# Two transformer blocks on one core: the FFN gate copied ahead of up, the sum of squares split, two weight splits swapped

## What is computed

```
def swiglu(h, w_gate, w_up, w_down):
    return (jax.nn.silu(h @ w_gate) * (h @ w_up)) @ w_down

def rms_norm(x, g):
    xf = x.astype(jnp.float32)
    y = xf * lax.rsqrt(jnp.mean(xf * xf, axis=-1, keepdims=True) + NORM_EPS)
    return (y * g.astype(jnp.float32)).astype(x.dtype)
...
        x = x + 0.5 * rms_norm(swiglu_2(rms_norm(x, g[0]), ffn_w_in[i, 0], ffn_w_out[i, 0]), g[1])
        ...
        x = x + rms_norm(m, g[3])
        x = x + 0.5 * rms_norm(swiglu_2(rms_norm(x, g[4]), ffn_w_in[i, 1], ffn_w_out[i, 1]), g[5])
```

## Time and profile before

| | |
|---|---|
| median of 3 runs | 2837.49 us (2835.84 to 2841.38) |
| the profiled execution | 2834.45 us, its span 2832.7 us |
| mean granted TensorE clock | 0.981 |
| busy: PE, DVE, ACT, POOL | 94%, 65%, 52%, 6% of the span |
| L671, L675 (in), L684 and L714 (out) | the FFN's matmuls |
| DVE L433 (`lo_a`) and L444 (`lo_b`) | 711.2 and 268.0 us busy |
| ACT L421 (`hi_a`) and L440 (`hi_b`) | 590.7 and 229.1 us busy |

### The profile page before, as it was taken

The page is one execution under the profiler, slowest core; times in us unless marked ns, Lnnn a source line. Parts: engine busy times, 40 slices in busy tenths (PEclk is TensorE's granted clock), DMA queues, the critical chain, the costliest instruction groups (busy, mean ns, idle before and its releaser), DMA issues.

```text
span 2832.7 us, 43885 instructions
## 1 busy us (share of the span) xinstructions
PE 2675.4 (94%) x15554; PEld 2305.1 (81%) x15554; DVE 1844.0 (65%) x2617; ACT 1459.1 (52%) x2295; POOL 160.5 (6%) x231
## 2 busy tenths in 40 slices
PE   6899998999899989999998899999999999999998
PEld 6888888888788868888887578888887888887787
DVE  4766667666666676666664566676656666666665
ACT  3545445454454465555543554555555545455644
POOL 0000000000000030000000300000011000003000
PEclk9999998999999999999998999999999999999999
DMA  4346642466666536656654056756535665653664
GB/s 128 104 149 195 183 129 90 148 186 183 188 178 182 153 128 178 188 167 198 188 167 152 1 161 187 204 160 195 158 126 175 196 191 173 184 169 114 178 186 134
DMA packets 575822, 457.02 MB, mean 161 GB/s; under 512 B 19276, under 2 KB 537956, under 8 KB 575716
## 3 DMA queue, kind: packets, MB, share of 16 engines
q1 hardware_dynamic: 573124, 453.47, 54.0%
q10 hardware_dynamic: 2560, 2.10, 0.3%
q0 software_dynamic: 32, 0.02, 0.0%
HBM read 452.37 MB, written 1.07 MB: 160 GB/s over the span
## 4 chain that ended last, share of the span: by engine, by line
issue 79%; PE 8%; DVE 5%; ACT 2%; POOL 2%; DVEq 1%; POOLq 1%; DMA 1%; SPq 0%; ACTq 0%
DVE lo_a L433 2%; POOL arena L1138 1%; POOL small L2091 1%; ACT hi_a L421 1%; POOLq L2090 1%; PE gu L872 1%; DVE small L1105 1%; PE gu L874 1%; PE gu L873 1%; PE gu L1330 0%; DVEq L1467 0%; PE gu L880 0%; PE gu L879 0%; PE gu L878 0%; PE gu L1332 0%
## 5 line engine op out<-in xcount | busy, mean ns | idle before, releaser
L433 DVE TENSOR_TENSOR lo_a<-raw_a,hi_a 128x2048 fp32r<-128x2048 f32 (+1 forms) x313 | 711.2, 2272 | 387.2 <-ACT hi_a L421 385.8
L421 ACT ACTIVATE hi_a<-raw_a 128x2048 fp32r<-128x2048 f32 (+1 forms) x313 | 590.7, 1888 | 140.5 <-PE acc L1360 28.2
L671 PE MATMUL tp<-xT,hi_a 128*128 128x512 f32 x1760 | 441.3, 393 | 0.0
L671 PE MATMUL gu<-xT,hi_a 128*128 128x512 f32 x1600 | 397.9, 391 | 0.0
L671 PEld LDWEIGHTS tp<-xT,hi_a 128*128 128x128 f32 x1760 | 324.5, 189 | 62.5
L671 PEld LDWEIGHTS gu<-xT,hi_a 128*128 128x128 f32 x1600 | 294.0, 188 | 56.9
L684 PE MATMUL acc<-hi_b,h_hi 128*128 128x512 f32 x800 | 313.8, 392 | 0.0
L684 PE MATMUL acc<-lo_b,h_hi 128*128 128x512 f32 x800 | 313.7, 392 | 0.0
L684 PE MATMUL acc<-hi_b,h_lo 128*128 128x512 f32 x800 | 311.2, 389 | 0.0
L444 DVE TENSOR_TENSOR lo_b<-raw_b,hi_b 128x1024 fp32r<-128x1024 f32 x220 | 268.0, 1218 | 6.7 <-ACT hi_b L440 6.7
L675 PEld LDWEIGHTS tp<-xT,lo_a 128*128 128x128 f32 x1760 | 240.1, 191 | 30.1 <-DVE lo_a L433 13.6
(11 more groups left out here) (316 smaller groups left out, 4168.1 us busy)
## 6 DMA issues: line engine op xcount, KB each, us to landing
raw_a<-in_ffn_w_in SPq DMA_DIRECT2D x352, 512.0 KB, 5.6
raw_b<-in_ffn_w_out SPq DMA_DIRECT2D x176, 512.0 KB, 3.6
raw_a<-in_w_in SPq DMA_DIRECT2D x52, 512.0 KB, 4.8
raw_a<-in_w_gate SPq DMA_DIRECT2D x44, 512.0 KB, 4.8
raw_a<-in_w_up SPq DMA_DIRECT2D x44, 512.0 KB, 6.1
raw_b<-in_w_down SPq DMA_DIRECT2D x44, 512.0 KB, 3.6
raw_a<-in_w_out SPq DMA_DIRECT2D x24, 512.0 KB, 4.2
raw_a<-in_c_w_in SPq DMA_DIRECT2D x24, 512.0 KB, 4.6
```

The source lines that it names most:

```text
L421: nc.scalar.activation(a_view(hi_a, par)[:, :, 0:width], a_view(raw_a, par)[:, :, 0:width], ACT.Copy).then_inc(a_hi, 1)
L433: nc.vector.tensor_tensor(a_view(lo_a, par)[:, :, 0:width], a_view(raw_a, par)[:, :, 0:width], a_view(hi_a, par)[:, :, 0:width].bitcast(F3 ...
L671: nc.tensor.matmul(banks[:, e, :], w_hi[:, kt, e * P:(e + 1) * P], xT[:, :, kt, :], start=(kt == 0), stop=False)
```

## The change

Three edits.

1. In an FFN tile, the copy of both halves (L736) becomes two copies of 256 columns. ACT now waits for `gate_done`, which PE raises after the last gate matmul, copies the gate half, waits for the scaled gate, takes Silu, then waits for `a_used`, copies the up half and goes on as before. DVE waits for `gate_part` ahead of the gate add and for `up_part` ahead of the up add.
2. In `post_pool` and `post_act`, POOL adds eps to the first half's sum as soon as that half is squared; ACT, after its second square and the drain that was already there, adds the second half with a one-column Identity activation (bias as the other addend); POOL then only raises to -0.5.
3. In `pre_dve`, `lo_slot_a` of the second slot stands ahead of `lo_slot_b` of the first down slot.

```
@@ pre_dve @@
             ins.then_inc(diag_ready, 1)
+            ahead_a(lo_slot_a, dve, s.a0 + 1)
             if s.kind == "ffn":
                 lo_slot_b(dve, s.b0, 0)
-            ahead_a(lo_slot_a, dve, s.a0 + 1)
@@ post_act @@
                 act.drain()
+                act.wait_ge(post_part, 2 * s.post + t + 1)
+                nc.scalar.activation(msy[:, t:t + 1], ssy[:, 2 * t + 1:2 * t + 2], ACT.Identity, bias=ssy0[:, t:t + 1]).then_inc(post_sum, 1)
@@ first_products, and the same in ffn_in_pe @@
+                            if s.kind == "ffn" and part == 2 and kt == KT - 1 and e == 0:
+                                mm.then_inc(gate_done, 1)
@@ ffn_tile_act @@
-            act.wait_ge(a_used, n + 1)
+            act.wait_ge(gate_done, m + 1)
             if not isinstance(m, int) or m >= 2:
                 act.wait_ge(hid_ready, m - 1)
-            nc.scalar.activation(parts[:, pm, :, :], (gu, tp)[pm][:, :, 256:512], ACT.Copy).then_inc(hid_part, 1)
+            nc.scalar.activation(parts[:, pm, 0, :], (gu, tp)[pm][:, 0, 256:512], ACT.Copy).then_inc(gate_part, 1)
             act.wait_ge(hid_scaled, m + 1)
             nc.scalar.activation(sg[:, pm, :], gs[:, pm, :], ACT.Silu).then_inc(hid_gate, 1)
+            act.wait_ge(a_used, n + 1)
+            nc.scalar.activation(parts[:, pm, 1, :], (gu, tp)[pm][:, 1, 256:512], ACT.Copy).then_inc(up_part, 1)
             act.wait_ge(hid_ready, m + 1)
@@ ffn_tile_dve @@
-            dve.wait_ge(hid_part, m + 1)
+            dve.wait_ge(gate_part, m + 1)
             nc.vector.tensor_tensor(gs[:, pm, :], banks[:, 0, 0:256], parts[:, pm, 0, :], ALU.add)
             dve.drain()
             nc.vector.tensor_tensor(gs[:, pm, :], gs[:, pm, :], rb, ALU.mult).then_inc(hid_scaled, 1)
+            dve.wait_ge(up_part, m + 1)
             nc.vector.tensor_tensor(parts[:, pm, 1, :], banks[:, 1, 0:256], parts[:, pm, 1, :], ALU.add)
@@ post_pool @@
             for t in range(NT):
-                pool.wait_ge(post_sq, 4 * s.post + 2 * t + 2)
-                rsqrt_pool(pool, rstdy[:, t:t + 1], 2 + t, ssy[:, 2 * t:2 * t + 1], eps_y[:, t:t + 1] if s.kind == "ffn" else EPS2,
-                           ssy[:, 2 * t + 1:2 * t + 2]).then_inc(rstdy_ready, 1)
+                pool.wait_ge(post_sq, 4 * s.post + 2 * t + 1)
+                nc.gpsimd.tensor_scalar(ssy0[:, t:t + 1], ssy[:, 2 * t:2 * t + 1], eps_y[:, t:t + 1] if s.kind == "ffn" else EPS2,
+                                        0.0, ALU.add, ALU.add).then_inc(post_part, 1)
+                pool.wait_ge(post_sum, 2 * s.post + t + 1)
+                nc.gpsimd.tensor_tensor(rstdy[:, t:t + 1], msy[:, t:t + 1], mhalf[:, 0:1], ALU.pow).then_inc(rstdy_ready, 1)
```

More of the change, by code:

```diff
@@ L295, in build_block @@
         ms = sm(8)
+        ssy0, msy = sm(2), ms[:, 2:4]
         rstd = sm(8)
@@ L331, in build_block @@
         scratch_out, scratch_in = sem("scratch_out"), sem("scratch_in")
-        out_done, post_sq = sem("out_done"), sem("post_sq")
+        out_done, post_sq, post_part, post_sum = sem("out_done"), sem("post_sq"), sem("post_part"), sem("post_sum")
         sq_act, diag_ready, rb_ps, rb_ready, rstd_ready, rstdx_ready, rstdy_ready, rstdf_ready = sem("sq_act"), sem("diag_ready"), sem("rb_ps"), sem("rb_ready"), sem("rstd_ready"), sem("rstdx_ready"), sem("rstdy_ready"), sem("rstdf_ready")
@@ L335, in build_block @@
         turned, turn_hi, turn_lo = sem("turned"), sem("turn_hi"), sem("turn_lo")
-        hid_part, hid_scaled, hid_gate, hid_ready, hid_hi, hid_lo = sem("hid_part"), sem("hid_scaled"), sem("hid_gate"), sem("hid_ready"), sem("hid_hi"), sem("hid_lo")
+        gate_done, gate_part, up_part, hid_scaled, hid_gate, hid_ready, hid_hi, hid_lo = sem("gate_done"), sem("gate_part"), sem("up_part"), sem("hid_scaled"), sem("hid_gate"), sem("hid_ready"), sem("hid_hi"), sem("hid_lo")
         gain_full = sem("gain_full")
@@ L676, in ffn_in_pe @@
                                           stop=(kt == KT - 1))
+                if e == 0:
+                    mm.then_inc(gate_done, 1)
             mm.then_inc(a_used, 1)
@@ L2084, in norm_y_dve, with rsqrt_pool @@
             ins.then_inc(yn_ready, 1)
-        def rsqrt_pool(pool, rs, at, ss, eps, more=0.0):
+        def rsqrt_pool(pool, rs, at, ss, eps):
             n = rs.shape[1]
-            nc.gpsimd.tensor_scalar(ms[:, at:at + n], ss, eps, more, ALU.add, ALU.add)
+            nc.gpsimd.tensor_scalar(ms[:, at:at + n], ss, eps, 0.0, ALU.add, ALU.add)
             pool.drain()
```

## The result

The changed kernel takes 2897.11 us (median of four runs, 2894.31 to 2899.15), the kernel before 2836.66 us beside it (four runs, 2833.52 to 2841.38). The ratio is 1.0221, with a 95% interval of 1.0209 to 1.0233: 60 us slower. The forecast was 2883, in a range of 2848 to 2908, with 0.85 on slower. The profiled execution took 2898.46 us; its span is 63.9 us longer than that of before.

The account below looks back on a forecast made before the run. The prediction took PE's matmuls to bound the loop. Its terms, -10.2 + 43 + 5 + 10 - 2 = +45.8 us on the profiled 2834.45, gave 2880.3; with 3.0 for the median, 2883, range 2848 to 2908.

Parts of the forecast that it names:

- What bounds the kernel: FFN loop: matmuls on PE bound it at 8.31 us a tile; the ACT and DVE ring takes 7.47, 0.84 less.
- forecast case: Whole kernel: the main outcome, slower, at 2867 to 2897 us, given a chance of 0.50.
- The swap: Stage starts, split order on DVE: PE's wait for lo_a shrinks and its first out comes sooner, -10.2 us over ten stages.
- The ring: ACT and DVE steps from one gate add to the next: 8.25 us instead of 7.47, a loop pair 16.71 against PE's 16.62.
- The drift in the loop: Loop tiles: 0.09 us lost a pair over 9 pairs, less the stage's starting margin; 0.5 a stage, +5 us.
- the rival with a longer ring: Loop tiles cost 0.1 us more than taken, PE loses it directly, +20 us: 2897 to 2925, chance 0.16.
- The last wait: Stage end: h of the last tile late by 6.2 us instead of 1.57 in nine stages, about 7 in one; +43 us.
- The clock: After PE's long idles at stage ends: half speed, 1.5 us lost each time; +10 us, bounds 0 and 16.
- The sum of squares: Before DVE's products: the power starts 0.24 us sooner in 8 FFN stages; -2 us, bounds -4 and +3.
- The figures of the Trainium skill: ACT's copies: cutting one adds an estimated 0.14 us a tile, off the path; up copy 399 ns, 0.02 longer, sum about 2 higher.

Follow-up runs that it names:

- part3: The kernel before with only the swap in pre_dve (lo_slot_a of the second slot ahead of lo_slot_b); 2818.07 us, ratio 0.9952.
- dose1: part3 with one more DVE addition, never read, in each FFN tile between lo_slot_a and lo_slot_b; 2824.33 us, ratio 0.9969.
- dose2: part3 with two more DVE additions, never read, in each FFN tile between lo_slot_a and lo_slot_b; 2863.17 us, ratio 1.0106.
- warm: The full change with 24 unread matmuls more (11 in the last stage) on PE ahead of its last wait; 2882.66 us, ratio 1.0175.
- upfirst: The full change with ACT's up copy put ahead of Silu in every tile; 2809.51 us, ratio 0.9912.
- part1: The kernel before with only the copy split into gate and up halves; 2901.94 us, ratio 1.0248.
- best_b: best_a with DVE's lo_slot_b moved from the tile's end to between scale and multiply; 2807.42 us, ratio 0.9905.
- best_a: upfirst with the sum-of-squares edit undone; 2808.71 us, ratio 0.9912.

## Why the prediction was right, step by step

- **What bounds the kernel.** PE's order of in and out and a ring beside it with 0.84 us of slack: borne out. part3, dose1 and dose2 walk along that slack and find its end. The time, 2897.11, lies in the stated range, but 14 us above the forecast and just over the upper end of the forecast case (2897).
- **The swap.** -10.2 forecast, -9.6 measured in the full change, where PE's first out waits for h (0.56 in the first stage, 0 to 0.87 in the ten), as forecast. With the old ring (part3) it doesn't, and the swap alone gives some 15 us.
- **The ring.** 8.25 forecast outside the loop, 8.33 measured; the pair 16.71 forecast, 16.78 measured. The mechanism was right and one term mis-sized. From the up add's start to the multiply's I took 0.50 (the add and its drain), and in the loop 0.16 and 0.05 more, 0.66 and 0.55. It was 0.66 in all loop tiles of nine stages (in the first stage 0.66 and 0.60 by turns; 229.23 to 229.90 above), and 0.60 outside the loop, though Silu was long done. Only in the first two tiles of the program is it 0.50, and the ring there 8.23, against the 8.25 forecast; these are the two tiles whose multiply doesn't also wait for `hid_lo` and `hid_hi`. Two more semaphores, long since raised, would then cost 0.10 behind a drain. That fits all tiles outside the loops, but no run was made for it, and what makes the loop tiles another 0.06 longer is open. In the kernel before this time passed while DVE waited for Silu in any case, so no row of before showed it. Elsewhere the sum held: Silu to up copy 0.33, up copy to up add 0.40 for 0.38 and 0.03.
- **The drift in the loop.** +5 forecast, +14.8 measured, for the same 0.07 a pair: a pair is 0.16 longer than PE's and not 0.09 (0.11 in the first stage); nine pairs in ten stages are about 14 against 8.1, and the margin at the start that I took off was there in two stages only, the sixth and the eighth. Of the 18 us by which the sum fell short of the profiled difference (45.8 against 63.9) this is 10; the matmuls behind the wait and the time between the stages are 4 together, the last waits and part 2 are 2 each. It is also why the time stands at the edge of the rival with a longer ring, 2897 and up.
- **The last wait.** 6.2 in nine stages forecast, 5.97 to 6.01 in eight measured. These are two measures of one thing: the 6.2 counts from the end of nine matmuls at 0.228, as the 1.57 of before did (from the rows it is 1.60), and so counted 390.08 is late by 6.17. Two stages came out differently, and nearly cancel, which is luck. The last one has 2.92, as the ring is shorter without a next slot, which I had overlooked. The second has 11.41 and not 7. There SP's loads stand behind one that waits for `lo_b`:

```profile
745.52 0.35 SPq L821 DMA_DIRECT2D raw_b<-in_w_down  x1
...
747.01 4.47 SPq L817 DMA_DIRECT2D raw_a<-in_ffn_w_in  x1
```

```profile
756.39 0.42 ACT L751 ACTIVATE h_hi<-arena 128x256 fp32r<-128x256 f32 x1 [1.09 <-DVE arena L770]
762.11 1.91 ACT L422 ACTIVATE hi_a<-raw_a 128x2048 fp32r<-128x2048 f32 x1 [5.31 <-DMA raw_a<-in_ffn_w_in]
```

The later ring released the slot later, the loads were issued 6.5 us later than before (738.99 there), 4.3 later as seen from PE's last group, and ACT waited 5.31 us for the data, where it had waited 4.12. Of those 4.12 the old ring had passed on 3.4 to PE's last wait (4.82 against 1.42 elsewhere); of the 5.31 it now passed on 5.4 (11.41 against 6.0), all of it.

- **The clock.** +10 forecast, 13 to 15.5 measured by warm. It also lasts longer than the 3.14 us of the earlier trace rows: 4.4 and 4.6 us in the windows above. The 5 us that come back between the stages were not foreseen.
- **The sum of squares.** -2 forecast, 1.0003 measured. ACT's addition took 0.29 us, and from the end of the second square's sum to DVE's start there are 1.12 us instead of 1.28 (third FFN stage). 0.16 us in eight stages is 1.3 us, too little for these runs. The prediction's own numbers, 0.25 and 0.1 from the end of the read at 965.47, give 965.82 and not 965.85 for the power; it changes nothing.
- **The figures of the Trainium skill.** By the Trainium skill, VectorE: DVE Perf Modes (The TRN2 errata), cutting a copy from PSUM costs a fixed 172 cycles again, an estimate of 0.14 us. The trace agrees: 0.363 and 0.367 us for the halves against 0.598 for the whole, 0.13 more. That it would cost the path nothing by itself is what upfirst showed. The Trainium skill's ScalarE: Activation LUTs (What ACT_TABLE_LOAD costs) gives 399 ns for the up copy, as an estimate; it took 367, so the 0.02 a tile that I set aside for it was rightly left out (0.04 a pair over 90 pairs would have been nearer 4 us than the 2 stated).

## What to carry to other kernels

When two engines hand a tile back and forth, add up the ring from one step to the same step of the next tile, in each engine's queue order, and compare it with the bound engine's time for a tile: above it every tile pays, just below it lateness is never made good and the stage's end pays it whole, and with some tenths of slack extra work is nearly free. An operation that is cut in two to start sooner should have both halves ahead of whatever waits for the other engine; queued behind it, the second half turns from hidden work into a link of the ring. Idle time of the other engine inside a ring can be filled by moving work into it, with nearly the same gain (2813.06 against 2809.51 us).

## What was not expected of the hardware

- From the up add to the multiply, behind a drain, DVE took 0.50 us in the two tiles with one semaphore wait there, 0.60 in those with three (all long satisfied) and 0.66 in the loops, where the row says only "issue" or, as in the earlier trace rows, names another engine. That the waits are the cause is the reading that fits, and not shown by a run. A tile of this loop runs 0.14 longer than one written out (7.62 and 7.48, 7.95 and 7.81, 8.29 and 8.15 us, where the ring ran free).
- One operation on one column is dear: ACT's Identity on 128x1 took 0.29 us (all 24 of the full change), against 0.36 for 256 columns from PSUM.
- Idle times of 1.42 us in PE's last wait had no fall of the clock in the 4 us behind them in these traces, one of 1.79 in dose1 and all of 3.8 and more were. One of 2.92 was in the full change, and one of the same length in part1 was not.
- Executions of one kernel can differ by how often the clock falls outside the FFN stages. best_b's profiled execution took 2816.66 us at a mean granted clock of 0.979, its three others 2805.99 to 2808.81 at 0.982 and 0.983. Its last waits are 0.37 or 0.38 but for the second stage (4.59), and of its 118 us at the low clock 105 lie outside the FFN stages, where best_a has 88.
